# Attention heads with every engine's order rewritten, and late modulation in pieces of 2048 columns

## What is computed

```
for i in range(DEPTH):
    sh1, sc1, g1, sh2, sc2, g2 = split(silu(c) @ ada_w[i] + ada_b[i])
    hx = rmsnorm(x) * (1 + sc1) + sh1
    yx = attention(hx, hc) if i == 0 else fourier(hx)
    x = x + g1 * yx
    x = x + g2 * conv_ffn(rmsnorm(x) * (1 + sc2) + sh2)
...
q, k, v = low-rank projections; q and k also get a rotary part
s = qn @ kn.T + qr @ kr.T
p = softmax(s * SM_SCALE)
o = p @ v, then y = concat(o) @ w_o
```

## Time and profile before

| what | us |
|---|---|
| median of 3 runs | 2379.08 |
| lowest and highest run | 2375.71, 2379.11 |
| the profiled execution's own time | 2378.23 |
| its span in the trace | 2376.4 |
| PE busy in the span | 2227.1 (94%) |
| DVE busy | 1759.1 (74%) |
| ACT busy | 1120.2 (47%) |
| POOL busy | 149.4 (6%) |
| bytes moved | 547.03 MB, mean 230 GB/s |

### The profile page before, as it was taken

The page is one execution under the profiler, slowest core; times in us unless marked ns, Lnnn a source line. Parts: engine busy times, 40 slices in busy tenths (PEclk is TensorE's granted clock), DMA queues, the critical chain, the costliest instruction groups (busy, mean ns, idle before and its releaser), DMA issues.

```text
span 2376.4 us, 46892 instructions
## 1 busy us (share of the span) xinstructions
PE 2227.1 (94%) x17426; PEld 2134.3 (90%) x17426; DVE 1759.1 (74%) x2189; ACT 1120.2 (47%) x1455; POOL 149.4 (6%) x128
## 2 busy tenths in 40 slices
PE   6889788879899999999999999989999999999997
PEld 3468677769889999999999998989999999999997
DVE  4866776778888888878868886888886664445665
ACT  5554333333356666633335544336666664334542
POOL 0000000003300000000000040340000000000013
PEclk9999999989899999989989999989999999999999
DMA  8764444457867787779977782786875555555553
GB/s 314 264 218 127 168 169 151 169 184 272 299 212 274 280 284 273 270 260 370 375 272 274 274 270 75 265 300 226 280 263 185 186 184 172 186 185 183 186 185 124
DMA packets 149976, 547.03 MB, mean 230 GB/s; under 512 B 17040, under 2 KB 17552, under 8 KB 149648
## 3 DMA queue, kind: packets, MB, share of 16 engines
q1 hardware_dynamic: 149904, 546.04, 66.3%
HBM read 543.88 MB, written 2.10 MB: 230 GB/s over the span
## 4 chain that ended last, share of the span: by engine, by line
PE 78%; DVE 13%; issue 5%; ACT 2%; DMA 2%; DVEq 0%; POOL 0%; SPq 0%; ACTq 0%; POOLq 0%
PE bank L1185 23%; PE bank L1186 22%; PE bank L1187 22%; DVE acc L745 4%; DVE w_lo L720 2%; PE bank L1216 2%; DVE w_lo L777 2%; PE bank L1191 1%; PE bank L1192 1%; PE bank L1193 1%; PE bank L1405 1%; DMA ada<-ada_late 1%; PE bank L1250 1%; ACT prob L584 1%; DMA early<-weights 1%
## 5 line engine op out<-in xcount | busy, mean ns | idle before, releaser
L467 ACT CAST w_hi<-raw 128x1024 fp32r<-128x1024 f32 x624 | 651.9, 1049 | 585.4 <-PE bank L1187 537.9
L1185 PE MATMUL bank<-h_hi,w_hi 128*128 128x256 f32 x3216 | 909.7, 283 | 13.6 <-DVE w_lo L720 9.2
L1187 PE MATMUL bank<-h_hi,w_lo 128*128 128x256 f32 x3216 | 908.1, 282 | 0.0
L1186 PE MATMUL bank<-h_lo,w_hi 128*128 128x256 f32 x3216 | 908.0, 282 | 0.0
L720 DVE TENSOR_TENSOR w_lo<-raw,w_hi 128x1024 fp32r<-128x1024 f32 x624 | 757.7, 1226 | 185.8 <-ACT w_hi L467 185.7
L1185 PEld LDWEIGHTS bank<-h_hi,w_hi 128*128 128x128 f32 x3216 | 611.2, 190 | 14.3 <-issue 14.3
L1186 PEld LDWEIGHTS bank<-h_lo,w_hi 128*128 128x128 f32 x3216 | 611.2, 190 | 0.3 <-issue 0.2
L1187 PEld LDWEIGHTS bank<-h_hi,w_lo 128*128 128x128 f32 x3216 | 610.8, 190 | 0.0
L745 DVE SCALAR_TENSOR_TENSOR acc<-ada,silu_c,acc 128x1024 f32<-128x1024 f32 x320 | 420.1, 1361 | 9.4 <-issue 7.0
L1185 PE MATMUL bank<-a_hi,w_hi 128*128 128x256 f32 x1408 | 395.1, 281 | 1.7 <-DVE a_lo L724 1.7
L1186 PE MATMUL bank<-a_lo,w_hi 128*128 128x256 f32 x1408 | 395.2, 281 | 0.0
(11 more groups left out here) (183 smaller groups left out, 2390.7 us busy)
## 6 DMA issues: line engine op xcount, KB each, us to landing
raw<-weights SPq DMA_DIRECT2D x626, 512.0 KB, 4.4
ada<-ada_late SPq DMA_DIRECT2D x320, 512.0 KB, 4.8
early<-weights SPq DMA_DIRECT2D x80, 512.0 KB, 4.7
ctx_s<-ctxT SPq DMA_DIRECT2D x1, 2048.0 KB, 9.1
x<-xT SPq DMA_DIRECT2D x1, 2048.0 KB, 15.1
outT<-h_pre SPq DMA_DIRECT2D x4, 512.0 KB, 2.6
dft_s<-dft SPq DMA_DIRECT2D x1, 768.0 KB, 4.7
conv_s<-conv SPq DMA_DIRECT2D x2, 176.0 KB, 3.5
```

The costliest lines, as they stand in the source:

```text
L467: act.copy(w_hi[:, slot, :], raw[:, slot, :]).then_inc(hi_done, 1)
L1185: pe.matmul(out, wh, hi_part, start=first, stop=False)
L1186: pe.matmul(out, wh, lo_part, start=False, stop=False)
L1187: return pe.matmul(out, wl, hi_part, start=False, stop=last)
```

## The change

In the heads, the function `step` of each engine is replaced by a loop over n with a new order:

- DVE: the inversion of the sums (now line 982) comes first in a pass, ahead of all modulation pieces. The diagonals are no longer made on DVE. The second maximum of a head stands behind the split of a chunk (`head_split(c + 5)`); the low part of a head's output is made one pass later. The maximum is written negated, so that line 940 goes away. `SM_SCALE` is applied to the queries instead (lines 952, 958 and 964, which become scalar_tensor_tensor).
- ACT: makes the diagonals (line 607), first in its pass, and copies `qraw` (line 589); the high part of a head's output is made one pass later. `qn_hi` is a multiplication by `SM_SCALE` (line 584).
- PE: the same steps in the same order. The semaphore `proj_taken` is split into one per operand, so each step waits for its own bank; T of head 8 waits for `mods(0)` as well.
- Late modulation everywhere: pieces of 128 x 2048 (1 MB) in a ring of two buffers in the same memory, one instruction and one DMA where there were two. In the heads three pieces go with an even pass, spread over it, and one with an odd pass. The first piece of each of the first two blocks is a multiplication without an addition, so `clear_accs(0)` and `clear_accs(1)` go away.
- SP follows the new order of DVE.

```
+ARING = 2
...
             def follow_ada(a, slot):
 
-                if isinstance(a, int) and a + RING >= N_ADA:
+                if isinstance(a, int) and a + ARING >= N_ADA:
                     return
                 sp.wait_ge(ada_used, a + 1)
-                sp.dma_start(ada[:, slot, :], one(ada_late[bass.ds(a + RING, 1), :, :].rearrange("o p n -> p o n")))\
+                sp.dma_start(ada[:, slot, :], one(ada_late[bass.ds(a + ARING, 1), :, :].rearrange("o p n -> p o n")))\
                     .then_inc(ada_in[slot], 16)
...
+            for n in range(HEADS):
+                a, c = 4 * (n // 2), head_chunk(n)
+                if n % 2:
+                    follow_ada(a + 3, 1)
+                else:
+                    follow_ada(a, 0)
+                    follow_ada(a + 1, 1)
+                if c + 4 <= C_WO + 3:
+                    follow_split(c + 4, (c + 4) % RING)
+                if n % 2 == 0:
+                    follow_ada(a + 2, 0)
+                if c + 5 <= C_WO + 3:
+                    follow_split(c + 5, (c + 5) % RING)
...
+            def diagonals(n):
+
+                act.wait_ge(rinv_done, n + 1)
+                for qt in range(2):
+                    act.mul(diag[:, qt, :], ident, rinv[:, qt:qt + 1]).then_inc(diag_done, 1)
+
...
             for n in range(HEADS):
-                step(n, n % 4, (n + 1) // 2, (n > 13) + (n > 14) - 1, C_WO + 3)
+                c, more, j = head_chunk(n), n + 1 < HEADS, n // 2 + 1
+                diagonals(n)
+                if n % 2 and more:
+                    rope_take(j)
+                if n:
+                    out_high(n - 1)
+                if n % 2:
+                    head_split(c + 4)
+                if more:
+                    keys_high(n + 1)
+                if n % 2 and more:
+                    rope_high(j)
+                if more:
+                    queries_high(n + 1)
+                if n % 2 == 0:
+                    head_split(c + 4)
+                probs_high(n)
+                if n % 2 == 0 and n + 2 < HEADS:
+                    v_high(j, 0)
+                    v_high(j, 1)
+                head_split(c + 5)
+                if more:
+                    exps(n + 1)
...
             def ada_step(b, k, e, a):
 
-                both = ADA_BLOCKS[b][1] == 2
-                width = 4 if both else 2
-                slot = e % RING
-                dve.wait_ge(ada_in[slot], 4 * (a - slot) + 16)
-                if not (isinstance(a, int) and a < width):
-                    dve.wait_ge(ada_used, a - width + 1)
-                acc = (acc0, acc1)[(e % width) // 2]
-                part = acc[:, (e % 2) * CH:(e % 2 + 1) * CH]
-                dve.scalar_tensor_tensor(part, ada[:, slot, :], one(silu_c[:, bass.ds(k, 1), 0:1]), part,
-                                         ALU.mult, ALU.add).then_inc(ada_used, 1)
+                width, slot = ADA_BLOCKS[b][1], e % ARING
+                dve.wait_ge(ada_in[slot], 8 * (a - slot) + 16)
+                acc, col = (acc0, acc1)[e % width], one(silu_c[:, bass.ds(k, 1), 0:1])
+                if isinstance(a, int) and a in (ADA_AT[B_DQKV], ADA_AT[B_HEADS]):
+                    dve.tensor_scalar(acc[:, :], ada[:, slot, :], col, None, ALU.mult).then_inc(ada_used, 1)
+                    return
+                dve.wait_ge(ada_used, a - width + 1)
+                dve.scalar_tensor_tensor(acc[:, :], ada[:, slot, :], col, acc[:, :], ALU.mult, ALU.add)\
+                    .then_inc(ada_used, 1)
...
-            def maxima(n):
-
-                for qt in range(2):
-                    dve.wait_ge(s_done, 2 * n + qt + 1)
-                    dve.reduce_max(mx[:, qt:qt + 1], bank[4 + qt][:, :], axis=AX.X).then_inc(mx_done, 1)
-                    dve.wait_ge(mx_done, 2 * n + qt + 1)
-                    dve.tensor_scalar(negmax[:, qt:qt + 1], mx[:, qt:qt + 1], -SM_SCALE, None, ALU.mult)\
-                        .then_inc(negmax_done, 1)
-
...
+            def queries_low(m):
+
+                dve.wait_ge(qn_hi_done, m + 1)
+                dve.scalar_tensor_tensor(qn_lo[:, m % 2, :], bank[B_Q][:, 0:SEQ], SM_SCALE,
+                                         qn_hi[:, m % 2, :].bitcast(f32), ALU.mult, ALU.subtract).then_inc(qn_taken, 1)
...
+            def maximum(n, qt):
+
+                dve.wait_ge(s_done, 2 * n + qt + 1)
+                dve.reduce_max(negmax[:, qt:qt + 1], bank[4 + qt][:, :], axis=AX.X, negate=True).then_inc(negmax_done, 1)
+
+            def inverse(n):
+
+                dve.wait_ge(exp_done, 2 * n + 2)
+                dve.reciprocal(rinv[:, :], psum_row[:, :]).then_inc(rinv_done, 1)
...
+            for n in range(HEADS):
+                c, more, j, a = head_chunk(n), n + 1 < HEADS, n // 2 + 1, 4 * (n // 2)
+                inverse(n)
                 if n == HEADS // 2:
                     mods(0)
...
+                if n % 2 == 0:
+                    head_ada(a)
+                    if n:
+                        out_low(n - 1)
+                    if more:
+                        keys_low(n + 1)
+                        queries_low(n + 1)
+                    head_ada(a + 1)
+                    probs_low(n, 0)
+                    probs_low(n, 1)
+                    head_split(c + 4)
+                    if n + 2 < HEADS:
+                        v_low(j, 0)
+                    head_ada(a + 2)
+                    if n + 2 < HEADS:
+                        v_low(j, 1)
+                    if more:
+                        maximum(n + 1, 0)
+                    head_split(c + 5)
+                    if more:
+                        maximum(n + 1, 1)
+                else:
+                    head_ada(a + 3)
+                    out_low(n - 1)
+                    if more:
+                        rope_cos(j)
+                    head_split(c + 4)
+                    if more:
+                        keys_low(n + 1)
+                        rope_sin(j)
+                        queries_low(n + 1)
+                        rope_low(j)
+                    probs_low(n, 0)
+                    probs_low(n, 1)
+                    if more:
+                        maximum(n + 1, 0)
+                    head_split(c + 5)
+                    if more:
+                        maximum(n + 1, 1)
+            out_low(HEADS - 1)
...
                         m, c = 2 * i + t, c0 + 4 * i + 2 * t
-                        for e in range(2):
-                            ada_step(b, m, 2 * t + e, ADA_AT[b] + 4 * i + 2 * t + e)
+                        ada_step(b, m, t, ADA_AT[b] + 2 * i + t)
...
             for n in range(HEADS):
-                step(n, n % 4, (n + 1) // 2, (n > 13) + (n > 14) - 1)
+                j, more = n // 2 + 1, n + 1 < HEADS
+                if n == HEADS // 2:
+                    ada_sum(0)
+                if n % 2 and more:
+                    rope_queries(j)
+                if more:
+                    keys(n + 1)
+                if n % 2 and more:
+                    rotate(j)
+                if more:
+                    queries(n + 1)
+                if n == HEADS // 2:
+                    pe.wait_ge(mod_done, MODS_EARLY + 1)
+                transposes(n)
+                if n % 2 == 0 and n + 2 < HEADS:
+                    values(j, 0)
+                    values(j, 1)
+                if more:
+                    scores(n + 1)
+                outputs(n)
...
-    late = _np.empty((N_ADA, P, CH), _np.float32)
+    late = _np.empty((N_ADA, P, D), _np.float32)
     for b, (first, n) in enumerate(ADA_BLOCKS):
-        late[ADA_AT[b]:ADA_AT[b + 1]] = rows[first:first + n].transpose(1, 0, 2, 3, 4).reshape(-1, P, CH)
+        late[ADA_AT[b]:ADA_AT[b + 1]] = rows[first:first + n].transpose(1, 0, 3, 2, 4).reshape(-1, P, D)
```

More of the change, by code:

```diff
@@ new lines, in probs_low, with out_low, head_split @@
+            def probs_low(n, qt):
+                dve.wait_ge(pt_hi_done, 2 * n + qt + 1)
+                lo_of(pt_lo[:, :, qt * P:(qt + 1) * P], bank[6 + qt][:, :].rearrange("p (t n) -> p t n", t=4),
+                      pt_hi[:, :, qt * P:(qt + 1) * P], pt_ready)
+            def out_low(n):
+                dve.wait_ge(o_hi_done, n + 1)
+                lo_of(row(h_lo, n), bank[3][:, 0:SEQ], row(h_hi, n), o_taken)
+            def head_split(c):
+                if c <= C_WO + 3:
+                    split(c, c % RING)
@@ L1357, in scores, with rotate @@
-            def scores(n, s):
-                buf, pair = s % 2, (s // 2) % 2
-                pe.wait_ge(proj_taken, 4 * n + 5 - s % 2)
+            def rotate(j):
+                pe.wait_ge(rq_taken, j + 1)
+                pe.matmul(bank[B_R][:, 0:SEQ], rot, qraw[:, :], start=True, stop=True).then_inc(rot_done, 1)
+            def scores(m):
+                buf, pair = m % 2, (m // 2) % 2
+                pe.wait_ge(kn_taken, m + 1)
+                pe.wait_ge(qn_taken, m + 1)
+                if m % 2 == 0:
+                    pe.wait_ge(qr_ready, m // 2 + 1)
```

(2 more changed lines are left out.)

352 lines of the change are left out of this document (139 added, 213 removed).

## The result

The changed kernel takes **2306.7 us** (median of 4 runs, 2302.5 to 2315.8), against 2379.1 for the kernel before: ratio 0.970, 95% interval 0.967 to 0.973. The forecast was 2303, range 2294 to 2328. The profiled execution took 2306.9 us, its span is 2305.0 (before: 2378.2 and 2376.4), a gain of 71.4 us where 75.1 were forecast.

The account below looks back on a forecast made before the run. The order on DVE, not any engine's amount of work, was taken to bound a pair of heads. Heads -64.6, their end -6.9 and the products -3.6 sum to -75.1 from 2378.2: 2303 us, range 2294 to 2328.

Parts of the forecast that it names:

- A: Rival: DVE bounds the heads, delays recur each pass, 2.7 us a pair, 2323 us in all; chance 0.18.
- B: Rival: a misplaced hand-over gives each pass in the heads a wait of about 2.3 us, 2338 us; chance 0.06.
- C: Rival: with the ring of two, pieces land late in two products and the down-projection; slower, up to 2476; chance 0.02.
- my 3.0 and 6.2: Heads: bounds in us for a 1 MB DMA, at 354 GB/s and at the heads' mean 169 GB/s.
- (2): End of the heads, after head 15's scores: 17.90 us long, to shrink to 11.0, a gain of 6.9 us.
- now DVE's maximum has no split ahead: 0.9 after S: End of the heads: first step, maximum 0.9 us after S, then exponential 1.7, inversion 1.9, diagonal 2.4, T 4.4.
- the walk through a pair: Heads: one even and one odd pass followed in time on PE, DVE and ACT; PE never waits, 0.1 us to spare.
- Term (1): Heads up to the end of head 15's scores: 459.1 us against 523.7, a gain of 64.6 us.
- Term (3): Outside the heads: 2048 pieces save 1.8 us each in the w_o and Fourier layer products, -3.6 in all.
- the end "0" of the term: Products outside the heads: lower end, no gain, if POOL's contention grows with the piece; the other end was -7.0.
- Term (4): Edits that cost nothing, and head 0's preparation in another order on DVE and ACT: 0, between -1 and +1 us.

Follow-up runs that it names:

- the order alone: Kernel before with DVE's order of the changed kernel and SP's to match, all else as before except both maxima behind the split: 2331.4 us, ratio 0.9795.
- the bunched kernel: Changed kernel with two modulation pieces right behind the inversion in every pass, instead of three spread over the even pass and one in the odd: 2322.7 us.
- the second execution of the same kernel: The changed kernel, unaltered, run again beside the version with the rearranged end of the heads: 2303.7 us, ratio 0.9678 to the kernel before.
- The new end: Changed kernel with two late pieces moved behind head 15's inversion and low parts, and head 14's last split behind both maxima: 2299.3 us.
- halves: Changed kernel with each modulation piece done as two instructions of 1024 columns, same 1 MB transfers and ring of two: 2312.9 us, ratio 0.971.

## Why the prediction was right, and where it was not

**Right, by its own mechanism.** The order on DVE set the length of a pair, not the amount of work. The pair was forecast at 28.33 and 0.1 us, and is 28.27; DVE's part was forecast at 24.3, and is 24.46; the piece of 2048 at 2.35, and is 2.35. The wait of S for `qr_lo` in the odd pass was to be 0.1, and is 0.18. The last S was to end at 459.1; its last matmul starts at 457.0. Runs show that this order is the cause: in the kernel before, the move of the inversion alone takes 27.0 us off the stretch and the rest of the order another 23.6, and bunching the pieces in the changed kernel gives 22.7 back. Of the rivals, A (DVE becomes the bound) is what the kernels with the order alone and with bunched pieces show: S waits for `qr_lo` 1.8 and 2.4 us. The changed kernel stays 0.2 us short of it. I had it "DVE over 90% busy", and that sign would have misled: in the bunched kernel DVE is busy 77% of the stretch, and in the changed one 84%. B did not show: `pt_lo` is waited for once, 1.4 us at the end of the heads, as in the kernel before. C did not show: no DVE wait for a piece stands among its waits in the product, and a piece lands 4.8 us (median) after its issue in the heads, between my 3.0 and 6.2.

**The term that failed is (2), the end of the heads.** It was to shrink from 17.90 to 11.0 us; from the last S (457.2) to the start of the product (477.92) it grew to 20.7, 9.7 over the forecast. The step at fault is "now DVE's maximum has no split ahead: 0.9 after S". In the walk through a pair I had each pass with V; for n = 14 I took 5.65 us off PE and did not walk through DVE's queue again. In that queue a split from 457.09 and a piece from 458.22 stand ahead of both maxima, which start at 460.49. The forecast had T start 2.4 us after S; it starts 6.1 after it (463.34). The second part of the miss is that a wait of 4.4 us brings the clock down, and T, O and the sum run at the lower level: 3.78 + 6.82 against 1.95 + 3.63. In the second execution of the same kernel the sum is at full clock, and the product starts 16.3 us after the last S, which is 5.3 over the forecast and not 9.7: 3.7 from the order and most of the rest from T at half clock come each time, the slow sum does not. The new end shows both parts: with the piece and the split moved, the wait is 1.14 and T is back at 2.05.

**Term (1) was 1.9 us too small a gain:** the last S comes 66.5 us earlier (523.5 to 457.0), not 64.6, though the first came 1.1 late. K behind the sum at head 8 takes 2.88 us here (363.69 to 366.57) and not the 4.43 of the earlier trace rows: I had carried over a loss of clock that shows only in the kernels in which S waits longer in the odd passes.

**Term (3), the two products, was mis-sized:** -3.6 forecast, -1.0 and -1.3 measured. DVE's costliest groups in the product with `w_o` (busy us and mean ns of one behind the count), in the changed kernel:

```profile
L758 DVE TENSOR_TENSOR w_lo<-raw,w_hi 128x1024 fp32r<-128x1024 f32 x32 | 46.2, 1444 | 1.2 <-ACT w_hi L475 1.1
L781 DVE SCALAR_TENSOR_TENSOR acc<-ada,silu_c,acc 128x2048 f32<-128x2048 f32 x16 | 42.7, 2671 | 0.5 <-DVE acc L769 0.5
```

The same in the kernel with halves, where the means are those of the kernel before to 2 ns:

```profile
L786 DVE SCALAR_TENSOR_TENSOR acc<-ada,silu_c,acc 128x1024 f32<-128x1024 f32 x32 | 51.1, 1635 | 0.5 <-DVE acc L770 0.5
L759 DVE TENSOR_TENSOR w_lo<-raw,w_hi 128x1024 fp32r<-128x1024 f32 x32 | 39.2, 1225 | 0.8 <-ACT w_hi L476 0.7
```

Together they are busy 88.9 us in the one and 90.3 in the other, so 16 long pieces save 1.4 us and not the 2.1 I had. Two of 1.635, the second starting 0.08 before the end of the first, and the next as much before its end, are 3.11 us a tile; one of 2.67 is 2.59: 0.52 saved. But the splits went from 1.225 to 1.444 on average, and two of them give 0.44 back. In order of time it is every second split, the one behind the piece, that takes 1.76 us instead of 1.21. POOL's addition of the squares runs at that time, and it grew too. POOL's group in the product, in the changed kernel:

```profile
L450 POOL TENSOR_TENSOR sq<-sq,sqt 128x256 f32<-128x256 f32 x14 | 36.3, 2590 | 1.1
```

And with halves:

```profile
L451 POOL TENSOR_TENSOR sq<-sq,sqt 128x256 f32<-128x256 f32 x14 | 22.4, 1600 | 1.1
```

That is the contention I had put at the end "0" of the term, and the answer, -2.3, lies between that end and my figure. PE's wait for POOL's last square, 3.52 us in the earlier trace rows, is 2.4 here, and 3.5 with halves.

**Term (4)** was 0 ± 1 for the preparation, and that holds. The first S came 1.1 later, but the delay lies ahead of the preparation: from the first `mod` (59.5 us before, 60.4 now) to the first S it is 184.4 to 184.8 us in all ten profiles, while the first `mod` comes anywhere from 59.5 to 62.5. What I had at nothing and was not: -3.1, +1.4 and -3.9 us in the feed-forward parts, -5.6 in all. PE's idle time in each of these differs by 0.6 us at most. Around the sum behind the first up-projection the clock is 0.78 over 20.7 us in the kernel before:

```profile
1015.00:1035.70 20.70, 20.70 (x144) 20.70 (x143) 11.49 (x16) 7.61 (x11) 0.00 (x0) 0.78 0.60 213
```

And 0.88 at the same place of the changed kernel:

```profile
947.20:967.90 20.70, 20.70 (x161) 20.70 (x160) 12.63 (x18) 9.45 (x13) 0.00 (x0) 0.88 0.70 256
```

The up-projection's stretch is 391.0 to 391.1 us in all five profiles of kernels with pieces in one instruction, and 394.1 to 397.5 in the five with pieces of 1024, the kernel before among them. So this difference comes with the length of the piece, and by the rows it is one spell of low clock less. Over the whole up-projection, 1 less the granted clock times the length is 14.5 us before and 11.2 after, so that the clock explains most or all of the 3.1. How the piece brings that about stays open. The +1.4 goes with the piece as well: the stretch to `mod` in the second feed-forward part is 384.6 to 385.8 us in the five profiles with pieces in one instruction, and 383.2 in four of the other five (384.7 in the fifth). The -3.9 of the last stretch can't be put down to the change, since that stretch varies between executions of the changed kernel (384.9 and 393.6).

**The rule on multiplications.** The Trainium skill, "ScalarE: Activation LUTs", section "Rules for kernel authors", has them on VectorE. Its reason is the rate per element, given there for bf16. The traces agree with it in fp32: two diagonals take 0.48 us of DVE and 0.70 of ACT. They don't agree with its result: with the diagonals on DVE the stretch is 3.6 us longer, 2.2 of them because DVE's queue is what S waits for, the rest at the lower clock of K at head 8. The whole times can't be told apart.

In sum: -66.5 instead of -64.6 up to the last S, +2.8 instead of -6.9 behind it, -2.3 instead of -3.6 in the products, and -5.5 elsewhere, that no term had. Of these, the 3.1 of the up-projection are clock for the most part; the rest is no more than executions of one kernel differ by, or speaks against the long piece (+1.4). That the total was only 3.7 us off is in part luck: the first and the last of these covered a part of the second.

## What to carry to other kernels

Where two engines are each idle in part, follow one period in order of time and ask which instruction the other engine waits for last; put it first in its queue, and spread what nobody waits for over the rest. Do that walk again for the passes at either end, where an engine loses work and the other doesn't. Once the large wait is gone, look for the next one: each relief of the queue ahead of it counts only until that wait is at zero.
